# Hybrid encoder on one core: a semaphore for each setup load, the rows first in the queue, the rotation's angles behind the first norm

## The reference, cut to what matters

```python
def rotary_tables(positions, dtype):
    inv_freq = ROPE_THETA ** (-jnp.arange(0, ROPE_DIM, 2, dtype=jnp.float32) / ROPE_DIM)
    ang = positions.astype(jnp.float32)[..., None] * inv_freq
    cos = jnp.cos(ang)[:, :, None, None, :].astype(dtype)
    sin = jnp.sin(ang)[:, :, None, None, :].astype(dtype)

cos, sin = rotary_tables(positions, x.dtype)
for l in range(DEPTH):                                  # DEPTH = 2
    h = rmsnorm(x, norm1_g[l])                          # x: (1, 256, 1024)
    proj = h @ w_in[l]
    q, k, v, z, xbc, dt_raw, gate_logits = jnp.split(proj, SPLIT_POINTS, axis=-1)
    q = partial_rotary(q.reshape(b, s, ATT_HEADS, 2, ATT_HEAD_DIM), cos, sin)
    k = partial_rotary(k.reshape(b, s, ATT_HEADS, 2, ATT_HEAD_DIM), cos, sin)
    ...                                                 # attention, state-space mixer, gates
    x = x + (g_att * a_out + g_ssm * m_out) @ w_out[l]
    x = x + peer_ffn(rmsnorm(x, norm2_g[l]), ...)       # 16 of 16384 experts per head, gathered
return rmsnorm(x, final_g)
```

## Time and profile before

| | before |
|---|---|
| median of 3 runs (range) | 2439.73 us (2439.36 to 2442.9) |
| the profiled execution, its own time | 2441.23 us |
| its span, first to last instruction | 2439.4 us |
| mean granted TensorE clock | 0.984 |
| PE busy, share of the span | 2091.8 us, 86% |
| DVE, ACT, POOL busy | 1327.5, 757.3, 513.7 us |
| DMA moved | 705.32 MB, mean 289 GB/s |
| first matmul of the first projection (L408) | 30.02 us |

### The profile page before, as it was taken

One profiled execution on the slowest core, in us unless ns is written; L12 is line 12 of the kernel. 1 busy time (PEld: TensorE's weight loads), 2 busy tenths in 40 slices (PEclk: granted clock), 3 DMA queues, 4 the chain that ended last, 5 costly groups with the idle time before them and its releaser, 6 DMA issues.

```text
span 2439.4 us, 23166 instructions
## 1 busy us (share of the span) xinstructions
PE 2091.8 (86%) x8312; PEld 1338.0 (55%) x8312; DVE 1327.5 (54%) x3225; ACT 757.3 (31%) x2023; POOL 513.7 (21%) x550
## 2 busy tenths in 40 slices
PE   5999999899878787777789999999998888777776
PEld 5688888766334332222266888888663344322222
DVE  1276355417657666765413772653366667666744
ACT  2034246203332333233220432561133332333232
POOL 0000000003333333333200000000043333333331
PEclk9999999899999999999999999999999999999999
DMA  4333444438999999999913234434499999999996
GB/s 155 130 121 122 165 181 164 155 146 352 422 422 421 422 421 421 422 421 416 381 69 138 104 138 165 178 143 168 169 372 421 421 421 421 421 421 421 422 421 269
DMA packets 90403, 705.32 MB, mean 289 GB/s; under 512 B 10000, under 2 KB 10128, under 8 KB 15792
## 3 DMA queue, kind: packets, MB, share of 16 engines
q0 software_dynamic: 78400, 553.81, 55.0%
q1 hardware_dynamic: 11168, 146.36, 15.7%
q10 hardware_dynamic: 720, 3.67, 0.4%
HBM read 702.62 MB, written 1.18 MB: 289 GB/s over the span
## 4 chain that ended last, share of the span: by engine, by line
PE 55%; DMA 30%; DVE 7%; ACT 4%; issue 3%; POOL 2%; SPq 0%; DVEq 0%; POOLq 0%; ACTq 0%
DMA ring<-in_peer_uv,ex_i 29%; PE bank L408 22%; PE bank L682 11%; PE bank L393 7%; DVE ring L1349 4%; PE bank L623 3%; PE bank L590 2%; PE bank L435 2%; POOL ring L1431 2%; PE bank L567 2%; ACT diag L919 1%; PE bank L577 1%; ACT wgt L912 1%; PE bank L482 1%; PE bank L427 1%
## 5 line engine op out<-in xcount | busy, mean ns | idle before, releaser
L682 PE MATMUL bank<-ring,diag 128*128 128x512 f32 x2048 | 950.0, 608 | 264.0 <-ACT diag L919 263.7
L1349 DVE SCALAR_TENSOR_TENSOR ring<-ring,h 128x1024 f32<-128x1024 f32 x512 | 607.0, 1223 | 481.3 <-DMA ring<-in_peer_uv,ex_i 480.1
L682 PEld LDWEIGHTS bank<-ring,diag 128*128 128x128 f32 x2048 | 373.2, 191 | 812.1 <-ACT diag L919 432.3
L1431 POOL DMA_INDIRECT ring<-in_peer_uv,ex_i x512 | 494.9, 967 | 1047.2 <-PE bank L682 677.3
L408 PE MATMUL bank<-hT,w_ring 128*128 128x256 f32 x2560 | 563.8, 380 | 2.0 <-ACT hT L713 2.0
L408 PEld LDWEIGHTS bank<-hT,w_ring 128*128 128x128 f32 x2560 | 482.4, 190 | 72.4 <-issue 6.4
L906 ACT ACTIVATE gel<-act_u 128x2 f32<-128x2 f32 x256 | 52.0, 203 | 844.2 <-DVE ring L1349 840.6
L919 ACT ACTIVATE diag<-cst,wgt 128x128 f32<-128x128 f32 x512 | 177.5, 394 | 24.0 <-PE bank L682 15.8
L912 ACT ACTIVATE wgt<-gel,gate_w 128x1 f32<-128x1 f32 x512 | 122.9, 287 | 9.3
L1402 POOL DMA_DIRECT2D cs_rows_dram<-cs_rows x2 | 1.3, 662 | 580.0 <-DVE cs_rows L1122 580.0
L1077 DVE SCALAR_TENSOR_TENSOR c_tmp<-xbc,par_all,c_tmp 128x254 f32<-128x254 f32 (+1 forms) x256 | 112.3, 480 | 4.6
(11 more groups left out here) (192 smaller groups left out, 1703.8 us busy)
## 6 DMA issues: line engine op xcount, KB each, us to landing
w_ring<-in_w_stream SPq DMA_DIRECT2D x62, 2048.0 KB, 8.2
fbuf<-cs_rows_dram POOLq DMA_DIRECT2D x32, 512.0 KB, 5.9
wq<-in_w_stream SPq DMA_DIRECT2D x4, 2048.0 KB, 8.2
ring<-in_peer_uv,ex_i POOLq DMA_INDIRECT x512
out<-in_w_stream SPq DMA_DIRECT2D x2, 2048.0 KB, 12.6
keys<-in_keys_t ACTq DMA_DIRECT2D x2, 1024.0 KB, 4.7
x_tok<-in_x SPq DMA_DIRECT2D x1, 1024.0 KB, 5.3
g2row<-in_norm_rows ACTq DMA_DIRECT2D x2, 512.0 KB, 6.2
```

The costliest lines, as they stand in the source:

```text
L682: ins = pe.matmul(bank[b0 + n][:], diag[:, PAIR * (m % 2) + s, :], ring[:, slot, DM + n * 512:DM + (n + 1) * 512], start=False, stop=True, ...
L1349: ins = dve.scalar_tensor_tensor(out=row, in0=row, scalar=1.0, in1=h2[:, b, :], op0=ALU.mult, op1=ALU.mult, accum_out=act_u[:, b, PAIR * k ...
L1431: pool.indirect_dma_start(ring[:, PAIR * q + s, :], None, peer_uv, bass.IndirectOffsetOnAxis(ap=ex_i[:, b, j:j + 1], axis=0))\
```

## The change

Each setup load gets a semaphore of its own, and each engine waits for those that it reads. `x_tok` is issued first, then `cst` and `par_all`, then the first weight chunk; `pos_i` and `wdt_all` go behind that chunk and ahead of the second. The angles become a function `angles()`, which DVE calls once, behind the `xn` of the first layer; ACT computes `sin_t` and `cos_t` behind `gained` of the first layer. `trig` moves to an address of its own, since `xn` is now alive beside it. POOL waits for no load of the setup any more.

```diff
-        trig, _ = place(temps, "trig", [P, 4, SEQ])
+        trig, _ = place(temps + 9216, "trig", [P, 4, SEQ])
...
         def _(sync):
-            sync.dma_start(cst[:], consts).then_inc(setup_loaded, 16)
-            sync.dma_start(x_tok[:], x[0].rearrange("(b p) d -> p b d", p=P)).then_inc(setup_loaded, 16)
-            sync.dma_start(par_all[:], params.rearrange("l p n -> p l n")).then_inc(setup_loaded, 16)
-            sync.dma_start(pos_i[:], positions.broadcast_to([P, SEQ])).then_inc(setup_loaded, 16)
-            sync.dma_start(wdt_all[:], w_dt.rearrange("l p n -> p l n")).then_inc(setup_loaded, 16)
+            sync.dma_start(x_tok[:], x[0].rearrange("(b p) d -> p b d", p=P)).then_inc(x_loaded, 16)
+            sync.dma_start(cst[:], consts).then_inc(cst_loaded, 16)
+            sync.dma_start(par_all[:], params.rearrange("l p n -> p l n")).then_inc(par_loaded, 16)
...
                     if n >= 2:
                         sync.wait_ge(chunk_freed.sem, n - 1)
+                    if n == 1:
+                        sync.dma_start(pos_i[:], positions.broadcast_to([P, SEQ])).then_inc(pos_loaded, 16)
+                        sync.dma_start(wdt_all[:], w_dt.rearrange("l p n -> p l n")).then_inc(wdt_loaded, 16)
...
-            pe.wait_ge(setup_loaded, 80)
+            pe.wait_ge(cst_loaded, 16)
...
+                pe.wait_ge(wdt_loaded, 16)
                 for b in range(TB):
                     for k in range(KD):
                         ins = pe.matmul(bank[3][:, b * 2 * SH:(b + 1) * 2 * SH], hT[:, k, b * P:(b + 1) * P],
...
-            act.wait_ge(setup_loaded, 80)
-
-            act.wait_ge(trig_ready, 1)
-            act.activation(sin_t[:], trig[:, 2, :], ACT.Sin)
-            act.activation(cos_t[:], trig[:, 3, :], ACT.Sin).then_inc(tables_ready, 1)
-
-            act.wait_ge(tables_ready, 1)
...
                 squares(0, L, 0, TB)
+                if L == 0:
+                    act.wait_ge(par_loaded, 16)
+                    act.wait_ge(cst_loaded, 16)
                 act.activation(aneg[:], param("alog"), ACT.Exp).then_inc(alog_exp.sem, 1)
                 gained(0, "n1g", L)
+                if L == 0:
+                    act.wait_ge(trig_ready, 1)
+                    act.activation(sin_t[:], trig[:, 2, :], ACT.Sin)
+                    act.activation(cos_t[:], trig[:, 3, :], ACT.Sin).then_inc(tables_ready, 1)
...
-            dve.wait_ge(setup_loaded, 80)
...
+            def angles():
+
+                dve.wait_ge(cst_loaded, 16)
+                dve.wait_ge(pos_loaded, 16)
...
+            dve.wait_ge(x_loaded, 16)
             dve.nop().then_inc(x_ready.sem, 1)
+            dve.wait_ge(par_loaded, 16)
...
                     ins = dve.tensor_scalar(xn[:, b, :], x_tok[:, b, :], rstd[:, b:b + 1], None, ALU.mult)
                 ins.then_inc(xn_ready.sem, 1)
+                if L == 0:
+                    angles()
...
-            pool.wait_ge(setup_loaded, 80)
```

More of the change, by code:

```diff
@@ L243, in sem @@
             return Count(once(name), per_layer)
-        setup_loaded = once("setup_loaded")
+        x_loaded = once("x_loaded")
+        cst_loaded = once("cst_loaded")
+        par_loaded = once("par_loaded")
+        pos_loaded = once("pos_loaded")
+        wdt_loaded = once("wdt_loaded")
         chunk_loaded = [once(f"chunk_loaded{i}") for i in range(2)]
@@ L987, in _, with trig_do @@
-            dve.nop().then_inc(trig_ready, 1)
+            def angles():
+                dve.wait_ge(cst_loaded, 16)
+                dve.wait_ge(pos_loaded, 16)
+                done = [0]
+                def trig_do(ins):
+                    done[0] += 1
+                    ins.then_inc(trig_step, 1)
+                    dve.wait_ge(trig_step, done[0])
+                MAGIC = 1.5 * 2.0 ** 23
+                T1 = 6.28125
+                T2 = math.floor((2 * math.pi - T1) * 2 ** 20) / 2 ** 20
+                T3 = 2 * math.pi - T1 - T2
+                trig_do(dve.tensor_copy(trig[:, 0, :], pos_i[:]))
+                trig_do(dve.tensor_scalar(trig[:, 0, :], trig[:, 0, :], const("freq"), None, ALU.mult))
+                for side, quarter in ((2, 0.0), (3, 0.25)):
+                    trig_do(dve.tensor_scalar(trig[:, 1, :], trig[:, 0, :], 1.0 / (2 * math.pi), quarter, ALU.mult, ALU.add))
+                    trig_do(dve.tensor_scalar(trig[:, 1, :], trig[:, 1, :], MAGIC, None, ALU.add))
+                    trig_do(dve.tensor_scalar(trig[:, 1, :], trig[:, 1, :], -MAGIC, None, ALU.add))
+                    for n, t in enumerate((T1, T2, T3)):
+                        trig_do(dve.scalar_tensor_tensor(out=trig[:, side, :], in0=trig[:, 1, :], scalar=-t,
+                                                         in1=trig[:, 0 if n == 0 else side, :], op0=ALU.mult, op1=ALU.add))
+                    if quarter:
+                        trig_do(dve.tensor_scalar(trig[:, side, :], trig[:, side, :], math.pi / 2, None, ALU.add))
+                    trig_do(dve.tensor_scalar(trig[:, side, :], trig[:, side, :], 3.1415925, -3.1415925, ALU.min, ALU.max))
+                dve.nop().then_inc(trig_ready, 1)
```

## The result

The changed kernel takes 2425.68 us, the median of 6 runs (2422.61 to 2428.34), against 2440.19 (6 runs) for the kernel before: a ratio of 0.9938 with a 95% interval of 0.9925 to 0.9951, that is 0.6% or some 15 us (12 to 18). The forecast was 2426.2 in a range of 2423.2 to 2430.5, and faster.

What follows compares the result with a forecast made beforehand. PE held 55% of the chain of waits and DMA 30%; the change touched only the serial first 30 us. Projection start 30.02 to 15.74 saves 14.3: 2440.5 - 14.3 = 2426.2 us, range 2423.2 to 2430.5.

Steps and rivals of the forecast that it cites:

- The start of the projection: First layer's first projection on PE: starts at 15.74 us instead of 30.02.
- par, not x, sets the first norm: First norm: par's landing at 8.16 and four small steps put the root at 9.29; x's squares would allow 8.99.
- From the start of the root to the first matmul of the projection nothing changes: Root through xn, transposes and hT copies to the first projection: still 6.45 us.
- The first chunk: First weight chunk: lands at 13.5 to 14.8 us, at least 0.9 ahead of PE's need at 15.74.
- The cover of the angles: Angles and sines beside the first projection: first bank copy up to 1.1 us late, free while PE fills the other bank.
- threshold of 21.6 for pos: Latest landing of pos, in us, at which the delayed first bank copy would still not stop PE's third fill.
- Table loads: ACT at the start: each load costs 1.28 us, with root or sines directly behind; the added ones cost nothing.
- The rival by which a load costs 2.66 us: Root's table load behind the squares: root at 10.4, gain only 13.2 us, 2427.3 us; chance 0.03.
- Everything after that shifted: All work behind the first projection's start at 15.74 us comes earlier by the whole gain, 14.3 us.
- the clock: TensorE clock rival: more half-speed time later costs 29 us to cancel the gain, 38 more for 2445.4 or above; chance 0.02.
- The gain of 14.3: Whole saving in us, all ahead of the first projection's start; bounds 13.2 to 15.0, chance 0.87.
- The other rivals: Late first chunk, 2431.7 us (0.03); late angles, 2427.8 (0.02); gain lost later or slow loads still awaited, about 2440 (0.03).

Runs made afterwards that it cites:

- par behind: The changed kernel with the wait for par and the four small steps behind xn instead of ahead of rms; one run, 2426.95 us.
- the try: The changed kernel with x in two loads, early root table, small steps behind xn, hT copies split, early unused PE matmuls; 2428.25 us, ratio 0.9944.
- pos late: The changed kernel with pos and wdt loaded behind the second weight chunk; one run, 2419.49 us.
- old queue: The changed kernel with pos and wdt back ahead of the first weight chunk; one run, 2424.3 us.
- pos later: The changed kernel with pos and wdt behind the second weight chunk and one more unused 2 MB load; one run, 2421.02 us.

## Why the prediction was right

- **The start of the projection** was forecast at 15.74 and came at 15.87 and 16.09. The order of the chain was right: par, four small steps, rms, root, xn, transposes, hT. par landed at 8.17 (8.16 forecast; it was issued 0.09 us later than I assumed and took as much less) and the root started at 9.29, as forecast.
- **"par, not x, sets the first norm"** was half wrong. x landed at 5.65, 0.3 later than estimated, which made the two conditions equal; with par's wait gone the start didn't move (15.88), and with x second it moved by 1.3 us, some 0.5 of them because x landed late there. The sentence that moving x ahead buys only room for the squares stands; the room is all used.
- **"From the start of the root to the first matmul of the projection nothing changes"**: 6.58 us instead of 6.45, since the last transposes too were slow (3.65 us for the 16 instead of 3.47).
- **The first chunk** landed at 13.1 (13.5 to 14.8 forecast), **pos** at 15.0 (15.5 to 16.8), both a little sooner. ACT was free at 22.3, ahead of the first full bank; at its old place the chunk would have cost 0.9 us (0.7 forecast).
- **The cover of the angles** held, and with 4 us more of delay as well. The threshold of 21.6 for pos was not shown: the run that passed it had a slow projection.
- **Table loads**: 1.28 us, and root and sines directly behind them in every profile where they waited for nothing else. The rival by which a load costs 2.66 us (the Trainium skill, ScalarE: Activation LUTs, "What ACT_TABLE_LOAD costs") doesn't occur: the kernel with par behind has 8.02 + 1.28 = 9.30 and the root at 9.31.
- **"Everything after that shifted"** is the step that did not hold. In the profiled pair the shift was 14.15 us at P0, 12.4 at R (the slow matmuls), 13.8 at P1 and 15.5 at the end. The loss of 1.75 us was mine to foresee: the clock stood among the rivals only as a fall later on, not as a rise that may come later than the first matmul. What came back behind R, 3.1 us, is within the scatter of the columns on those stretches. The gain of 14.3 agrees with the measured 12 to 18 us; that the median came within 0.5 us of the forecast is partly luck, since the start cost 1.75 us that the forecast lacked, and in the profiled pair only the scatter behind it made up for them.

The other rivals did not come about: the chunks don't share the DMA engines (the second landed 8 us behind the first, behind pos and wdt), no engine waits for the slow loads, and the end moved with the start.

## What to carry to other kernels

One semaphore for several loads makes every engine wait for the last of them, and waits at the head of an engine's list can also hold back what needs no load at all, here a table load of 1.28 us. Follow the chain at a program's start in order of time and ask of each piece who reads it first; what is read 55 us later belongs behind the first matmuls, if the work queued behind it on its engine can be late without stopping another (here the copy of a bank, while PE fills the second bank). Then look for the second condition that is about to bind: here the squares with their table load lay 0.05 us under par, and the first weight chunk 2.7 us under the transposes.

## What the runs showed of the hardware

- TensorE's clock at the start of a program: of fourteen profiles, eight began the first projection with matmuls of 631 ns or so (one of them, the try, behind an idle time of 3.29 us) and six with 379 ns. Where PE's first work was the 16 transposes, the first rise, by the trace's record, came 3.1 to 3.6 us behind the first of them ("before" both times, "pos late", "old queue") or 7.8 to 9.4 us behind it (the seven slow ones, each with a gap of 0.93 us in PE's work ahead of the projection), never in between; a gap of 0.95 to 1.77 us behind an early rise did no harm. A slow start cost 1.6 to 2.4 us. Unused work on PE right ahead of the transposes, from 6.5 or 6.6 us on, brought the rise forward in both profiles that had it.
- The granted clock reads 1.00 in the slow stretch ahead of the first rise, where the trace has no record of it, and 0.50 in a slow stretch behind a fall. At a program's start the durations of the matmuls (631 or 379 ns, 421 or 272 ns for a transpose) tell the clock.
- A small load can land late: pos, 128 KB, landed 1.6 to 2.3 us behind the load ahead of it, par or a chunk of 2 MB, in twelve profiles. In "pos late" and "pos later", where only wdt stood behind it in the queue, it was 0.9 and 0.7 us; what makes the difference was not tested.
- Three chips gave the kernel before 2440.1, 2443.5 and 2440.4 us (17, 9 and 1 runs, which scatter over 6 to 8 us on one chip), so I compare only on one chip. What makes the stretch with the gathers 778 to 784 us long in the same code was not settled.
